# State-space outputs with channels on partitions, and a new placing of banks, loads and dense tiles in the third block's state-space stage

## The reference, cut to what matters

```python
def step(S, inp):                      # x (B,L,G,E,P), b, c (B,L,G,N), a (B,L,G,E)
    cum = jnp.cumsum(ai, axis=1)
    seg = cum[:, :, None] - cum[:, None, :]
    Lm = jnp.exp(jnp.where(mask, seg, -jnp.inf))
    cb = jnp.einsum('btgn,bsgn->btsg', ci, bi)
    y = jnp.einsum('btsg,btsge,bsgep->btgep', cb, Lm, xi)
    y = y + jnp.einsum('btgn,bgenp->btgep', ci, S) * jnp.exp(cum)[..., None]
    S_new = jnp.exp(cum[:, -1])[..., None, None] * S + ...
```

## Time and profile before

| | |
|---|---|
| median of 3 runs | 3759.87 us |
| the profiled execution: time | 3762.13 us |
| its span | 3760.0 us |
| mean granted TensorE clock | 0.936 |
| PE, DVE, ACT, POOL busy | 89%, 57%, 35%, 34-35% of the span |
| DMA | 438.53 MB, mean 117 GB/s |
| the stage changed | 2880.0 to 3305.0 us of the span |

### The profile page before, as it was taken

One profiled execution on the slowest core, in us unless ns is written; L12 is line 12 of the kernel. 1 busy time (PEld: TensorE's weight loads), 2 busy tenths in 40 slices (PEclk: granted clock), 3 DMA queues, 4 the chain that ended last, 5 costly groups with the idle time before them and its releaser, 6 DMA issues. The chain is left out here.

```text
span 3760.0 us, 44458 instructions
## 1 busy us (share of the span) xinstructions
PE 3335.2 (89%) x17680; PEld 2666.8 (71%) x17680; DVE 2129.8 (57%) x2550; ACT 1264.0 (34%) x1924; POOL 1310.6 (35%) x609
## 2 busy tenths in 40 slices
PE   7989998999898898988999789788977878789997
PEld 5767776888766678867888577557865646668885
DVE  6375955888755583445656547355985574531112
ACT  4223343323243322333323322233432354332222
POOL 3324343444332334343444333225620101134442
PEclk9989998999999999999999899889988878899999
DMA  3213353474332355443353224323322433322322
GB/s 112 84 58 119 123 176 119 154 249 148 140 97 78 102 138 163 148 143 124 131 172 105 86 89 138 97 66 116 110 87 95 151 96 115 108 81 92 102 84 69
DMA packets 219614, 438.53 MB, mean 117 GB/s; under 512 B 58592, under 2 KB 102304, under 8 KB 212624
## 3 DMA queue, kind: packets, MB, share of 16 engines
q1 hardware_dynamic: 212336, 425.21, 34.6%
q10 hardware_dynamic: 7072, 10.49, 0.7%
HBM read 386.39 MB, written 49.24 MB: 116 GB/s over the span
## 5 line engine op out<-in xcount | busy, mean ns | idle before, releaser
L356 POOL TENSOR_TENSOR third_feed_lo<-third_feed_raw,third_feed_hi 128x1024 fp32r<-128x1024 f32 (+3 forms) x191 | 441.8, 2316 | 1016.9 <-ACT third_feed_hi L349 1003.2
L356 POOL TENSOR_TENSOR second_feed_lo<-second_feed_raw,second_feed_hi 128x1024 fp32r<-128x1024 f32 (+3 forms) x182 | 404.8, 2225 | 664.1 <-ACT second_feed_hi L349 635.0
L356 POOL TENSOR_TENSOR first_feed_lo<-first_feed_raw,first_feed_hi 128x1024 fp32r<-128x1024 f32 (+4 forms) x182 | 395.6, 2178 | 601.9 <-ACT first_feed_hi L349 592.0
L349 ACT ACTIVATE third_feed_hi<-third_feed_raw 128x1024 fp32r<-128x1024 f32 (+3 forms) x191 | 190.9, 1001 | 311.4 <-PE ffn_low L275 79.1
L273 PE MATMUL third_in_ps<-third_in_h_hi,third_feed_hi 128*128 128x512 f32 (+1 forms) x584 | 243.1, 416 | 36.7 <-DVE third_in_h_lo L2982 19.2
L349 ACT ACTIVATE second_feed_hi<-second_feed_raw 128x1024 fp32r<-128x1024 f32 (+3 forms) x182 | 173.9, 956 | 211.1 <-PE ffn_low L275 70.8
L273 PE MATMUL mixer_acc<-first_h_hi,first_feed_hi 128*128 128x512 f32 x544 | 225.5, 414 | 13.0 <-DVE first_h_lo L428 7.8
L274 PE MATMUL third_in_ps<-third_in_h_lo,third_feed_hi 128*128 128x512 f32 (+1 forms) x584 | 235.2, 403 | 0.0
L275 PE MATMUL third_in_ps<-third_in_h_hi,third_feed_lo 128*128 128x512 f32 (+1 forms) x584 | 234.7, 402 | 0.0
L349 ACT ACTIVATE first_feed_hi<-first_feed_raw 128x1024 fp32r<-128x1024 f32 (+4 forms) x182 | 168.3, 929 | 190.4 <-PE mixer_acc L275 61.0
L518 DVE SCALAR_TENSOR_TENSOR ffn_ada_sum<-ffn_ada_w,cond,ffn_ada_sum 128x512 f32<-128x512 f32 x196 | 219.6, 1137 | 4.0
(11 more groups left out here) (775 smaller groups left out, 8412.0 us busy)
## 6 DMA issues: line engine op xcount, KB each, us to landing
third_feed_raw<-in_stream SPq DMA_DIRECT2D x156, 512.0 KB, 3.4
second_feed_raw<-in_stream SPq DMA_DIRECT2D x130, 512.0 KB, 3.5
first_feed_raw<-in_stream SPq DMA_DIRECT2D x120, 512.0 KB, 3.3
ffn_ada_w<-in_w_ada SPq DMA_DIRECT2D x48, 1024.0 KB, 5.3
ssm_seg<-scratch_cum SPq DMA_DIRECT2D x32, 512.0 KB, 6.0
scratch_gates<-mixer_gate ACTq DMA_DIRECT2D x32, 256.0 KB, 2.1
mix_gin<-scratch_gates SPq DMA_DIRECT2D x32, 256.0 KB, 3.2
first_feed_raw<-in_stream SPq DMA_DIRECT2D x28, 256.0 KB, 3.0
```

The lines of the kernel that those rows point to most:

```text
L349: self.nc.scalar.activation(self.hi[:, p % self.cut, :n], self.raw[:, p % self.deep, :n], ACT.Copy).then_inc(self.cut_hi, 1)
L356: eng.tensor_tensor(self.lo[:, p % self.cut, :n], self.raw[:, p % self.deep, :n], self.hi[:, p % self.cut, :n].bitcast(F32), ALU.subtract) ...
```

## The change

1. The inter and intra products swap their operands: the states and `xdt` are now the stationary side, c and the decays move. The result has channels on partitions: eight 128x128 inter matmuls a chunk for two of 128x512, and intra matmuls with a stationary 128x64 and 128 moving columns, whose outputs alternate between partitions 0 to 63 and 64 to 127. `turn`, `put_out` and `y_tok` go; `out` writes `y` itself.
2. exp(cum) is needed by channel. `stage_third_gates` computes it on 64x512 and stores it to DRAM (`ecum`); `load_e` loads it for each chunk, spread over 64 partitions a head, by four DMAs into a single buffer `e` (128 x 2 x 4 x 128), once `out` of the chunk before has read it. `etok` goes.
3. Gram and turned b move to banks 3 and 2, turned x to banks 4 and 5. The gram of the next group needs only the reads of chunk 2; x needs those of chunk 3. PE's inter product of chunk c >= 2 waits for DVE's reads of chunk c-2.
4. `gate(g-1)` is cut in two: tiles 0 and 1 before the mask of the gram, 2 and 3 behind the x products; their loads stand ahead of the x loads in SP's list.
5. `FILL3` is new, and `place` interleaves pieces 8 and 9, so that eight tiles of them need only group 0's outputs.

```diff
@@ stage_third_gates @@
+                sp.wait_ge(raised, 1)
+                sp.dma_start(dram["ecum"], sizes.work).then_inc(raised_out, 16)
                 rows_.sync(sp, many + 1)
...
+                rows_.scalar(act, many // 2 + 2)
+                act.wait_ge(sizes.summed, 2)
+                nc.scalar.activation(sizes.work, sizes.cum[:], ACT.Exp).then_inc(raised, 1)
                 rows_.scalar(act, many)
...
-                nc.scalar.activation(etok[:], cum_tok[:], ACT.Exp).then_inc(raised, 1)
@@ Branches @@
+    def place(self, t):
+        n = t - DT * DT
+        if 0 <= n < 2 * DT:
+            return DT + n // 4 % 2, n // DT * 4 + n % 4
+        return divmod(t, DT)
@@ FILL3 @@
-FILL3 = (((8, 8, 6, 6, 6, 6), (4, 4, 4, 4)), ((4, 4, 0, 0, 0, 0), (0, 0, 0, 0)),
-         ((0, 0, 0, 0, 0, 8), (6, 6, 6, 6)), ((8, 8, 8, 8, 0, 0), (0, 0, 0, 0)))
+FILL3 = (((8, 4, 4, 4, 4, 0), (4, 4, 2, 2)), ((8, 8, 6, 6, 0, 0), (4, 4, 0, 0)),
+         ((0, 0, 0, 0, 0, 0), (8, 8, 6, 6)), ((6, 6, 4, 4, 4, 4), (0, 0, 0, 0)))
@@ SP @@
+                def load_e(g, c):
+                    if 4 * g + c:
+                        sp.wait_ge(read, 8 * g + 2 * c)
+                    by = dram["ecum"].rearrange("(d g j k) t -> d g k j t", d=2, g=4, j=4)
+                    for d in range(2):
+                        for k in range(2):
+                            sp.dma_start(e[half(k), d], spread(by[d, g, k, :, c * P:(c + 1) * P], 64)
+                                         ).then_inc(e_in, 16)
...
                     dense.sync(sp, before(g, 0))
+                    if g:
+                        for j in range(2, 4):
+                            load_gate(g - 1, j)
                     load_x(g, 2)
                     load_x(g, 3)
                     dense.sync_gates(sp, pieces_by(g, 0, 0))
-                    if g:
-                        for j in range(2, 4):
-                            load_gate(g - 1, j)
...
-                    for n in range(4, 8):
-                        load_cum(g, n)
+                    load_cum(g, 4)
+                    load_cum(g, 5)
+                    load_e(g, 1)
+                    load_cum(g, 6)
+                    load_cum(g, 7)
                     dense.sync_gates(sp, before(g, 1))
                     dense.sync(sp, pieces_by(g, 1, 0))
                     dense.sync_gates(sp, pieces_by(g, 1, 0))
+                    load_e(g, 2)
                     dense.sync_gates(sp, pieces_by(g, 1, 1))
                     for j in range(2):
                         load_gate(g, j)
-                    for n in range(4 if g < 3 else 0):
+                    for n in range(2 if g < 3 else 0):
+                        load_cum(g + 1, n)
+                    load_e(g, 3)
+                    for n in range(2, 4 if g < 3 else 0):
                         load_cum(g + 1, n)
                     if g < 3:
                         load_start(g + 1)
+                        load_e(g + 1, 0)
@@ PE @@
-                        pe.wait_ge(read, 8 * g)
+                        pe.wait_ge(read, 8 * g - 2)
...
-                    if g:
-                        turn(g - 1, 3)
-                        pe.wait_ge(y_out, 4 * g)
...
                         if j >= 2:
                             pe.wait_ge(x_scaled, 8 * g + 2 * (j - 1))
+                        elif g:
+                            pe.wait_ge(read, 8 * g)
...
-                    fill(g, 0, 1)
+                        if j == 1:
+                            fill(g, 0, 1)
...
                         if c >= 2:
-                            pe.wait_ge(y_out, 4 * g + c - 1)
+                            pe.wait_ge(read, 8 * g + 2 * c - 2)
                         for d in range(2):
-                            last = nc.tensor.matmul(ps[:, 2 + 2 * (c % 2) + d], c_[:, g % 2, at], states[:, d, c], start=True,
-                                                    stop=True)
+                            for j in range(4):
+                                to = slice(j * P, (j + 1) * P)
+                                last = nc.tensor.matmul(ps[:, 2 + 2 * (c % 2) + d, to], states[:, d, c, to],
+                                                        c_[:, g % 2, at], start=True, stop=True)
...
-                            for e in range(8):
-                                last = nc.tensor.matmul(ps[:, 6 + c % 2, e * 64:(e + 1) * 64], seg[:, n % 4, e],
-                                                        xdt[:, d, c, e * 64:(e + 1) * 64], start=d == 0 and e == 0,
-                                                        stop=d == 1 and e == 7, skip_group_check=True)
+                            for i in range(8):
+                                last = nc.tensor.matmul(ps[half(i % 2), 6 + c % 2, i // 2 * P:(i // 2 + 1) * P],
+                                                        xdt[:, d, c, i * 64:(i + 1) * 64], seg[:, n % 4, i],
+                                                        start=d == 0 and i < 2, stop=d == 1 and i >= 6,
+                                                        skip_group_check=True)
                         fill(g, 1, c)
-                        if c:
-                            turn(g, c - 1)
-                turn(3, 3)
+                pe.wait_ge(read, 30)
@@ DVE, out(g, c) @@
+                    part = y[:, :, c * P:(c + 1) * P]
                     dve.wait_ge(inter_ready, 4 * g + c + 1)
+                    dve.wait_ge(e_in, 64 * (4 * g + c + 1))
-                    by_head(y_tok[:, c % 2], ps[:, 2 + 2 * (c % 2)], etok[:, c, head(0, g)]).then_inc(read, 1)
+                    v.tensor_tensor(part, by_channel(ps[:, 2 + 2 * (c % 2)]), e[:, 0], ALU.mult).then_inc(read, 1)
-                    by_head(tmp[:], ps[:, 3 + 2 * (c % 2)], etok[:, c, head(1, g)]).then_inc(read, 1)
+                    v.tensor_tensor(by_channel(tmp[:]), by_channel(ps[:, 3 + 2 * (c % 2)]), e[:, 1], ALU.mult
+                                    ).then_inc(read, 1)
...
+                    v.tensor_tensor(part, part, by_channel(tmp[:]), ALU.add).then_inc(added, 1)
...
+                    v.tensor_tensor(part, part, by_channel(ps[:, 6 + c % 2]), ALU.add).then_inc(y_made, 1)
@@ DVE, groups @@
+                    dense.vector(dve, before(g, 0))
+                    if g:
+                        gate(g - 1, (0, 1))
                     dve.wait_ge(grammed, g + 1)
...
+                        if j == 1:
+                            dense.vector(dve, pieces_by(g, 0, 0))
+                    if g:
+                        gate(g - 1, (2, 3))
...
-                    if g:
-                        gate(g - 1)
```

More of the change, by code:

```diff
@@ L3752, in pieces_by @@
         def pieces_by(g, part, k):
-            return tiles_by(g, part, k) // DT
+            return dense.whole(tiles_by(g, part, k))
         def before(g, part):
-            return sum(FILL3[a][b][c] for a, b, c in spots if (a, b) < (g, part)) // DT
+            return dense.whole(sum(FILL3[a][b][c] for a, b, c in spots if (a, b) < (g, part)))
         def head(d, g):
@@ L3964, in decay @@
                     act.wait_ge(cum_in[n % 4], 16 * (2 * g + n // 4 + 1))
-                    for e in range(8):
-                        at = 32 * (n % 2) + 8 * g + e
-                        last = a.activation(seg[:, n % 4, e], seg[:, n % 4, e], ACT.Relu, scale=-1.0,
+                    for i in range(8):
+                        at = 32 * (n % 2) + 8 * g + i
+                        last = a.activation(seg[:, n % 4, i], seg[:, n % 4, i], ACT.Relu, scale=-1.0,
                                             bias=cum_tok[:, n // 2, at:at + 1])
@@ L4183, in _ @@
                 dense.vector(dve, 2 * DT)
-                gate(3)
+                gate(3, range(4))
                 invert(3)
```

81 lines of the change are left out of this document (34 added, 47 removed).

## The result

The changed kernel took 3737.7 us, median of four runs (3736.8 to 3745.4), beside 3760.4 for the kernel before: a ratio of 0.9938, 95% interval 0.9922 to 0.9954, so 23 us less where the forecast had 47. The measured time lies inside the range and on the side that had 0.87, but only half of the forecast gain came.

The account below looks back on a forecast made before the run. A chain of handovers bounds the state-space stage, no engine full. Output halves -3.1, preparing halves -9.3, -8.8, -2.6, -21.5, tail -1.4 sum to -46.7 us; 3762.1 - 46.7 - 2.3 = 3713 us, range 3685 to 3748.

Parts of the forecast that it names:

- the side that had 0.87: Whole kernel: chance 0.87 of being faster than the kernel before, against 0.06 for same and 0.07 for slower.
- the new filling in group 1: Group 1's preparing half: 28 dense tiles instead of 8, yet 36 us against 44.8, -8.8.
- Swapped operands: Output chunks: 32 intra records take 2.0 us instead of 3.49, about 1.5 us a group; inter equal, no drain.
- Turn and copy gone: Output halves: 64 transposes, 16 copies and their handovers go, and with them the 4.94 us TensorE pause and its likes.
- The transfer of e: Output halves: four exponent DMAs a chunk into one buffer, 6.5 us from read to landing, bounds 4 and 9 us.
- What is ahead of load_e(3) in SP's queue counts: Output halves of groups 0 and 2: evictions and six issues delay exponents; +5.6 us in group 0, group 2 near 48.
- x(2) is issued only after gate 1, at about T+5: Preparing half: x tile 2 asked for about 5 us after VectorE finishes the previous group's last output chunk, landing 4.9 later.
- The new filling, group 0: Group 0's preparing half: 24 dense tiles instead of 40, 47.6 to 38.3 us, -9.3.
- Earlier gates: Preparing halves: with gates split, sums start at once behind the first two products; group 2 from 39.6 to 37 us, -2.6.
- two thirds of a microsecond for wake-ups: Output halves of groups 1 to 3: two thirds of a microsecond on top of cold inter and intra products, +2.9 together.
- the queue eats most of it: SP's waits ahead of exponents delay the next group's exponents and x, 3 us in eight other stretches: +24, 3737; chance 0.14.
- their waits at 20: Output halves: 2.5 us at each of 8 exposed exponent transfers, 20 us; hidden transfers would give 3693 us, chance 0.2.

Follow-up runs that it names:

- experiment 1: Changed kernel with fifteen of the sixteen blocks of exponent loads (60 DMAs) left out: 3713.0 us, 0.9872.
- experiment 2: Changed kernel with a second place for the exponents and every load one chunk earlier: 3733.8 us, 0.9921.
- experiment 10: Changed kernel with SP's list reordered, x and gated norm tiles first: 3732.9 us with one place for the exponents, 3714.1 us with two.
- experiment 9: Two places for exponents, their DMAs on POOL's queue: 3737.3 us, on ACT's: 3725.3; rows of 2048 bytes on SP's: one place 3738.4, two places 3727.7.

## Why the prediction was half right

The two steps that failed are the new filling in group 1 and, in group 2, what stands ahead of the loads of `e` in SP's queue: 11.0 and 8.3 of the 30.4 us.

- *Swapped operands*: right. 1.90 us for 32 records (2.0 forecast), inter unchanged. The Trainium skill, "TensorEngine Tiling (Array Packing)", Key Properties, has a drain at each change of mode; 0.34 us to the next start against 0.32 shows none of a size that counts here.
- *Turn and copy gone*: right, the 53.1 us of ACT's waits and the 4.94 us pause have no successor.
- *The transfer of e*: right in size where the queue was quiet, about 6.3 us from read to usable in group 1 (3043.4 to 3049.7), 6.5 forecast. Directly behind two loads of cums it took 8.8 us from the first issue to the first use in group 0 (2954.1 to 2962.95) and 9.9 in group 2 (3130.9 to 3140.8). DVE's waits before out(3) in groups 1 and 3 were 4.9 and 5.0 us (6 to 7 forecast), before out(2) none and 0.6 (1 forecast).
- *"What is ahead of load_e(3) in SP's queue counts"*: right in group 0, where e(3) was asked for 5.6 us after out(2) had read, as forecast; the 3.3 us over come mostly from the longer transfer. In group 2 the step failed. It counted evictions and gate loads and left out the feed loads, which also stand ahead of e(2) and took 11.8 us. So e(2) was asked for at M+29.3 in place of M+21.5 and e(3) at M+43.9 in place of M+36.4, and the half took 56.3 in place of 48 us.
- *"x(2) is issued only after gate 1, at about T+5"*: right in the changed kernel, where it was asked for at T+4.4, T+4.0 and T+5.7; in group 2 x was turned at T+9.5 (T+10 forecast), and that half took 34.7 us (37 forecast). It no longer holds once the output halves are shorter: then x(2) went out at T+13 (experiment 1) and T+16 (experiment 2).
- *The new filling*: right in sign; undone it costs 11 us. Its size failed in group 1, forecast at 36 us (-8.8) and measured at 47.0 (+2.2). The working let 16 tiles run while DVE waits for `e` and x, with the first product at T+17.3. In its place PE stood 6.8 us in two waits for banks that DVE, busy with x, gates and weights, had not evicted, and the product began at T+23.0: 5.7 us. Products and sums took 1.4 us more than forecast with warm sums. Behind the sums come the other 3.9 us: the six tiles priced at 4.1 us took 6.6, at a granted clock of 0.50; in the kernel of experiment 10 the same six took 4.2 at 1.00. Taking the longer bank wait away shortened that half by 5 us in one profile and moved no median, so what the half is worth to the whole stays open.
- *The new filling, group 0*: 42.8 in place of 38.3 us. Ten tiles fewer ahead of the first product were priced at 6.9 us and gave 2.7, as x came later: PE turned it 23.0 us after the stage's start (2902.5) against 20.1 before, and the new block e(0) took 2.6 us of SP's queue ahead of it. With the DMAs of `e` on POOL's and on ACT's queue (experiment 9) DVE needed 31.2 and 32.1 us from its first instruction of this half to M, against 35.0 in the changed kernel and 34.0 with two places on SP's queue.
- *Earlier gates*: right, 9.4 us by the run that undid them.

In the output halves of groups 1 to 3 the forecast adds two thirds of a microsecond for wake-ups; no row and no run shows this term by itself.

The rival "the queue eats most of it" (3737 us, 0.14) gave the measured time, but not 3 us in each of eight stretches. The queue's share is some 3 us in group 0's preparing half, 3.3 in its output half and 8.3 in group 2's, about half of the 30.4; group 1's 11 us lie in PE's own list. That the rival's figure came out to the microsecond is in part luck.

The runs show this much: the exponents cost 24.7 us, where the forecast had priced their waits at 20; two places alone return 4, the order alone 5, both 23.6. That this kernel takes 3714 us, nearly the forecast 3713, is a coincidence, as it has a second place and another order. What the turn, the copies and the swap gave is not measured by itself. By difference it is an estimate: 23 gained and 24.7 paid, less the 11 of the table and 9.4 of the gates, leaves some 27 us, if the parts add up, and experiments 2 and 10 show that such parts need not. The new table in the kernel before was not tried.

## To carry to other kernels

A load that moves onto a busy queue has two prices, its own landing and the delay of all that stands behind it; count every issue and every wait in the queue from the last sure point to the load in question, feed loads too, and order the queue by when each tile is needed. Work that is put into an engine's gaps is not free: ask whether its bank is free by then, and price it at the clock that rows show for that place, here 1.1 us a dense tile (6.6 for six) in place of 0.69. Where a wait is removed and the time does not move, look whether the next stretch grew by the same amount: here some 29 us left the output halves and 23 came back before the next first mask. Two edits that are each worth 4 us may be worth 24 together when either wait hides the other.

## What was not expected of the hardware

- The time to issue was longer directly behind large loads. Four DMAs of `e` took SP 2.56 us on a quiet queue and 4.5 to 5.9 us right behind two 512 KB loads of cums; with a quarter of the rows it was 2.4 and 4.8 us (experiment 9).
- POOL issued one such DMA in 0.61 us, but with pauses of 1.4 to 7.9 us inside a block, so that a queue that stands idle was no better than the crowded one.
